# A transformer pair on one core: the second block's projections as four 2x2 block products of seven half-size products each

## The reference, cut to what matters

```
h = modulate(rmsnorm(x, norm1_g), sh_a, sc_a)             # 512 x 1024
proj = h @ w_in                                            # 1024 x 2080
q, k, v, g, a_low, p = split(proj, [256, 512, 1024, 1536, 1568])
la = log_sigmoid(a_low @ w_dec + b_dec) / 16               # decay, two directions
o = gated linear attention of q, k, v with la, in both directions
o = rmsnorm(o) * silu(g)
pooled = ((window mean - identity) of p) @ w_pool, scaled, for windows 2, 4, 8, 16
out = concat(o, pooled) @ w_out
```

## Time and profile before

| what | value |
|---|---|
| median of 3 timed runs | 1575.39 us (1570.91 to 1577.83) |
| span of the profiled execution, first to last instruction | 1569.6 us |
| own time of the profiled execution beside its span | not listed apart; the timed runs lie 1.3 to 8.3 us above the span |
| TensorE busy | 1407.1 us, 90% of the span |
| VectorE, ScalarE, GpSimd busy | 46%, 24%, 24% |
| mean granted TensorE clock | 0.977 |
| the stage of the change, 1005 to 1150 us: TensorE busy | 140.6 of 145 us |

### The profile page before, as it was taken

One profiled execution on the slowest core, in us unless ns is written; L12 is line 12 of the kernel. 1 busy time (PEld: TensorE's weight loads), 2 busy tenths in 40 slices (PEclk: granted clock), 3 DMA queues, 4 the chain that ended last, 5 costly groups with the idle time before them and its releaser, 6 DMA issues. The chain is left out here.

```text
span 1569.6 us, 21971 instructions
## 1 busy us (share of the span) xinstructions
PE 1407.1 (90%) x8518; PEld 948.7 (60%) x8518; DVE 717.6 (46%) x1222; ACT 375.2 (24%) x775; POOL 375.1 (24%) x293
## 2 busy tenths in 40 slices
PE   5998998999999989989999999999988977988781
PEld 4864444886454458778888868874667863333230
DVE  5261435124549977687615153500364464332224
ACT  3313445203343333332210032401231010000001
POOL 2420002620005525644545532000000011111110
PEclk9999999999999999999999999999999979999996
DMA  5238220123112114315242312421134169999995
GB/s 195 69 98 272 76 58 24 54 81 107 54 55 81 54 56 161 110 57 203 79 160 86 103 54 63 102 71 54 30 109 160 56 257 382 422 425 423 425 382 219
DMA packets 119831, 232.57 MB, mean 148 GB/s; under 512 B 13361, under 2 KB 103055, under 8 KB 110515
## 3 DMA queue, kind: packets, MB, share of 16 engines
q1 hardware_dynamic: 114403, 220.54, 39.0%
q0 software_dynamic: 5184, 8.55, 1.5%
q10 hardware_dynamic: 144, 2.10, 0.3%
HBM read 223.66 MB, written 17.84 MB: 154 GB/s over the span
## 5 line engine op out<-in xcount | busy, mean ns | idle before, releaser
L991 PE MATMUL psv<-arena 128*128 128x256 f32 x1328 | 291.6, 379 | 2.5 <-issue 2.5
L991 PEld LDWEIGHTS psv<-arena 128*128 128x128 f32 x1328 | 251.7, 190 | 39.1 <-issue 5.2
L953 PE MATMUL psv<-arena,wslot 128*128 128x512 f32 x384 | 170.8, 598 | 0.5 <-issue 0.5
L2322 DVE TENSOR_TENSOR arena<-arena,psv 128x512 f32<-128x512 f32 x82 | 56.4, 688 | 224.0 <-PE psv L991 222.1
L1589 PE MATMUL pss<-arena 128*64 128x512 f32 x432 | 119.4, 621 | 16.5 <-DMA arena<-w_expert_in 12.7
L953 PEld LDWEIGHTS psv<-arena,wslot 128*128 128x128 f32 x384 | 71.1, 190 | 84.0 <-issue 83.7
L1681 ACT ACTIVATE arena<-pss 128x512 f32<-128x512 f32 (+2 forms) x130 | 74.3, 571 | 193.7 <-PE pss L953 130.0
L953 PE MATMUL pss<-arena 128*128 128x512 f32 x224 | 99.6, 597 | 7.1 <-ACTq L155 4.5
L2537 DVE SCALAR_TENSOR_TENSOR arena<-psv,ccols,arena 128x510 f32<-128x510 f32 (+1 forms) x96 | 71.9, 749 | 52.8 <-ACT arena L1851 49.5
L1589 PEld LDWEIGHTS pss<-arena 128*64 128x64 f32 x432 | 36.8, 143 | 72.1 <-issue 72.1
L991 PE MATMUL psv<-arena,wslot 128*128 128x256 f32 x320 | 72.5, 381 | 6.1 <-ACT arena L1730 2.5
(11 more groups left out here) (362 smaller groups left out, 2150.4 us busy)
## 6 DMA issues: line engine op xcount, KB each, us to landing
arena<-w_expert_in SPq DMA_DIRECT2D x25, 2048.0 KB, 25.7
arena<-w_expert_out SPq DMA_DIRECT2D x32, 1024.0 KB, 29.6
wslot<-w_in SPq DMA_DIRECT2D x28, 1024.0 KB, 5.5
wslot<-w_ada SPq DMA_DIRECT2D x19, 1024.0 KB, 6.3
arena<-w_in SPq DMA_DIRECT2D x14, 1024.0 KB, 6.9
wslot<-w_expert_in SPq DMA_DIRECT2D x5, 2048.0 KB
arena<-w_ada SPq DMA_DIRECT2D x5, 1024.0 KB, 8.9
arena<-x SPq DMA_DIRECT2D x8, 512.0 KB, 7.5
```

What stands on the lines that cost most here:

```text
L953: m = mm(o, l, r, start=(n == 0), stop=(n == len(pairs) - 1))
L991: m = mm(o[:, j * HALF_T:(j + 1) * HALF_T], l[:, c, j * P:(j + 1) * P], r[:, c, :], start=new and j == 0 and c == 0, stop=j == 1 and c == ...
L2322: L.did(V.tensor_tensor(o, x, y, ALU.add), *sig)
```

## The change

The eight blocks are regrouped into four pairs: k with the first half of v (unit 17), the second half of v with the first half of p (unit 18), both of g (unit 19, feature-major), q with the second half of p (unit 20). Each runs through `seven` with the new buffers `part_c`, `held_c`, `term_c`. q leaves token-major into `q2tok` and is transposed by TensorE into `q2T`, as k was before. The activations' four terms are made by VectorE. a_low has its own buffer `wa2` and its load, ahead of the weight blocks, and runs behind unit 17; the decay matmuls run behind unit 20. The sums of weights for unit 17 straddle phase 4 on GpSimd: two of them before it, the in-place one behind it, since the context tiles still read that block. The `wdec` memset moves behind `last_part(17)`.

```diff
+        term_c = [at(B + (16 + 4 * n) * K, 4, HALF_T) for n in range(4)]
+        part_c = [at(147 * K, 4, WC), at(151 * K, 4, WC), at(115 * K, 4, WC)]
+        held_c = [at(119 * K + n * SEQ, 2, HALF_T) for n in range(4)]
+        wa2 = at(155 * K, KC, 32)
+        q2tok = at(24 * K, NT, WC)
...
-        for key, col, n in (("k2", O2_K, 256), (("v2", 0), O2_V, 256), (("v2", 1), O2_V + 256, 256), ("q2", O2_Q, 256),
-                            (("g2", 0), O2_G, 256), (("g2", 1), O2_G + 256, 256), ("a2", O2_A, 32),
-                            (("p2", 0), O2_P, 256), (("p2", 1), O2_P + 256, 256)):
-            stream(key, w2, col, n)
+        for key, col in ((("kv2", 0), O2_K), (("kv2", 1), O2_V), (("vp2", 0), O2_V + WC), (("vp2", 1), O2_P),
+                         (("g2", 0), O2_G), (("g2", 1), O2_G + WC), (("qp2", 0), O2_Q), (("qp2", 1), O2_P + WC)):
+            stream(key, w2, col, WC)
...
+        def corner_c(v, u, j, n):
+            o, c = {17: ((k2, 0), (v2, 0)), 18: ((v2, WC), (p2, 0)), 20: ((q2tok, 0), (p2, WC))}[u][j]
+            return o[:, 2 * n:2 * n + 2, c:c + WC]
...
-            stream_to("q2")
+            load(wa2, w2[:, O2_A:O2_A + 32].rearrange("(c p) n -> p c n", p=P), "ld_a2")
+            stream_to(("vp2", 1))
```

TensorE's list:

```diff
-            for t in range(NT):
-                L.need(s["h2_ready"])
-                L.need(s["half_ready"])
-                token_tile("s", wk, t, h2T)
-            used()
-            for t in range(NT):
-                token_tile("v", wv, t, h2T)
-            used()
-            L.need(s["k2_ready"], NT)
+            L.need(s["h2_ready"], 2)
+            L.need(s["half_ready"], 2)
+            seven(17, h2T, part_c, term_c, True, by_token=True, w=[wk, wv])
+            L.need(s["h2_ready"], 2)
+            L.need(s["half_ready"], 2)
+            pe.wait_ge(s["ld_a2"], 16)
+            for src, n in ((h2T, SEQ), (hcT, CTX)):
+                strips(bank("v"), wa2, src, n).then_inc(s["full_v"], 1)
+            pe.wait_ge(s["corner_ready"], 14)
+            pe.wait_ge(s["raw_ready"], 3 * 17 + 2)
             for j in range(2):
                 turn("s", [k2[:, t, j * P:(j + 1) * P] for t in range(NT)])
...
+            seven(18, h2T, part_c, term_c, by_token=True, w=[wv1, slot(("vp2", 1))])
+            seven(19, h2T, part_c, term_c)
+            seven(20, h2T, part_c, term_c, by_token=True)
+            pe.wait_ge(s["corner_ready"], 17)
+            pe.wait_ge(s["raw_ready"], 3 * 20 + 2)
             for j in range(2):
-                feature_tile("s", w, j, h2T)
...
+                turn("s", [q2tok[:, t, j * P:(j + 1) * P] for t in range(NT)])
+            pe.wait_ge(s["ld_small"], 16 * 10)
+            L.need(s["a2_ready"], 2)
+            for t in range(NT + NTC):
+                mm(bank("v"), a2T[:, t * P:(t + 1) * P], wdec, start=True, stop=True).then_inc(s["full_v"], 1)
+
+            pe.wait_ge(s["raw_ready"], 3 * 21)
```

GpSimd's list:

```diff
                 L.did(TT(part[0], a21, a22, ALU.add), s["part_ready"])
                 L.did(TT(part[1], part[0], a11, ALU.subtract), s["part_ready"])
+                unused()
                 L.did(TT(a21, a11, a21, ALU.subtract), s["part_ready"])
...
-            phase(4)
+            parts(17, part_c, lambda: phase(4))
+            last_part(17, part_c)
             nc.gpsimd.memset(wdec, 0.0).then_inc(s["wdec_zero"], 1)
+            for u in range(18, 21):
+                parts(u, part_c)
+                last_part(u, part_c)
```

VectorE's list, up to the end of unit 17:

```diff
-            for b2 in range(2):
-                for t in range(NT):
-                    b = full()
-                    L.did(V.tensor_copy(v2[:, t, b2 * 256:(b2 + 1) * 256], b[:, 0:256]), s["free_v"])
+            dve.wait_ge(s["half_ready"], 3 * NT + NTC)
+            term(term_c[0], quarter(h2T, 0, 1), quarter(h2T, 0, 0))
+            term(term_c[1], quarter(h2T, 1, 1), term_c[0])
+            term(term_c[2], quarter(h2T, 1, 1), quarter(h2T, 0, 1))
+            term(term_c[3], quarter(h2T, 1, 0), term_c[1])
+            add_second(17, held_c)
+            recombine(17, held_c, None, corner_c)
```

More of the change, by code:

```diff
@@ L470, in build @@
             half_ready row_ready sq_ready on_ready dz_ready mixT_ready sums_ready
[L471 to L472 removed]
+            x1_ready x1T_ready pinT_ready x2_ready mod_ready h2_ready hc_ready mT_ready
+            ld_a2 k2_ready a2_ready absz_ready lz_ready la_ready bexp_ready qb_ready kexp_ready kst_ready
             sprev_ready sc_ready o2_ready sq2_ready rt2_ready cat_ready x3_raw x3_ready h3_ready lg_ready
@@ L611, in build @@
                  ("dz", 0), ("dz", 2), ("gd", 0), ("gd", 2), ("brd", 0), ("brd", 2),
[1 row of a table removed]
[2 rows of a table added]
         SEVEN_JOB = [4, 7, 10, 14, 17, 20, 23, V_ON, V_ON + 3, V_ON + 14, V_ON + 17, V_ON + 20, V_ON + 23,
-                     V_ON + 26, V_ON + 29, V_ON + 32 + NT, V_ON + 35 + NT + NTC]
+                     V_ON + 26, V_ON + 29, V_ON + 32 + NT, V_ON + 35 + NT + NTC,
+                     V_ON + 38 + 2 * NT + 3 * NTC, V_ON + 43 + 2 * NT + 3 * NTC, V_ON + 46 + 2 * NT + 3 * NTC,
+                     V_ON + 49 + 2 * NT + 3 * NTC]
         TERM_SET = [("q", 0)] * 3 + [("h", 0)] * 2 + [("h", 1)] * 2 + [("q", 1)] * 4 + [("h", 2)] * 2 + \
-                   [("h", 3)] * 2 + [("h", 4)] * 2
+                   [("h", 3)] * 2 + [("h", 4)] * 2 + [("q", 2)] * 4
         def seven_slots(u):
@@ L682, in by4 @@
             return v.rearrange("p (h n) -> p h n", h=4)
-        S_NORM = 267
+        S_NORM = 259
         def chunk_at(d, n):
@@ L822, in _ @@
                          a["w_decay_2"][0, d], "ld_small")
-            stream_to(("p2", 1))
+            stream_to(("qp2", 1))
             for g in range(2, 4):
@@ L972, in token_tile, with seven @@
                     .then_inc(s["full_" + r], 1)
-            def seven(u, x, part, term, first=False, by_token=False, lower=lambda: None):
-                n = at_slot[0]
-                assert [n, n + 1] == seven_slots(u), (u, n)
+            def seven(u, x, part, term, first=False, by_token=False, lower=lambda: None, w=None):
                 assert jobs["v"] == SEVEN_JOB[u], (u, jobs["v"])
-                w = [slot((SEVEN[u][0], SEVEN[u][1] + j)) for j in range(2)]
+                if w is None:
+                    assert [at_slot[0], at_slot[0] + 1] == seven_slots(u), (u, at_slot[0])
+                    w = [slot((SEVEN[u][0], SEVEN[u][1] + j)) for j in range(2)]
                 a11, a12, a22 = w[0][:, 0:4, :], w[0][:, 4:8, :], w[1][:, 4:8, :]
@@ L1342, in _ @@
             L.need(s["half_ready"], NTC)
-            wk, wv = slot("k2"), slot(("v2", 0))
+            wk, wv = slot(("kv2", 0)), slot(("kv2", 1))
             for t in range(NTC):
@@ L1347, in _ @@
                 token_tile("v", wv, t, hcT)
-            wv1 = slot(("v2", 1))
+            wv1 = slot(("vp2", 0))
             for t in range(NTC):
@@ L1368, in _ @@
-            used()
-            w = slot("q2")
-            for j in range(2):
-                feature_tile("s", w, j, h2T)
[L1372 to L1393, removed]
@@ L1987, in _ @@
                 turned(h2T, t, gain[:, 0:8], mod[:, 0:8, 0])
-            for t in range(NT):
-                evict(k2[:, t, :], 256, "k2_ready")
+            hold_first(17, held_c)
+            corner_of(17, None, ACT.Copy, corner_c)
+            hold_third(17, held_c)
             for j in range(2):
                 evict(k2T[:, j, :], SEQ, "k2_ready")
+            hold_first(18, held_c)
+            hold_third(18, held_c)
+            corner_of(18, None, ACT.Copy, corner_c)
+            hold_first(19, held_c)
+            hold_third(19, held_c)
+            corner_of(19, g2T, ACT.Silu)
+            others_of(19, g2T, ACT.Silu, None)
+            hold_first(20, held_c)
+            hold_third(20, held_c)
+            corner_of(20, None, ACT.Copy, corner_c)
             for j in range(2):
                 evict(q2T[:, j, :], SEQ, "k2_ready", ACT.Copy, scale=DK2 ** -0.5)
-            for j in range(4):
-                evict(g2T[:, j, :], SEQ, "k2_ready", ACT.Silu)
             for t in range(NT + NTC):
@@ L2130, in weights_in, with parts @@
                 return w
-            def parts(u, part):
+            def parts(u, part, unused=lambda: None):
                 w = weights_in(u)
@@ L2800, in _ @@
                 L.did(V.tensor_copy(a2T[:, c0:c0 + n], b[:, 0:n]), s["a2_ready"], [s["free_v"]])
[L2801 to L2812, removed]
+            add_second(18, held_c)
+            recombine(18, held_c, None, corner_c)
+            add_second(19, held_c)
+            recombine(19, held_c, g2T)
+            add_second(20, held_c)
+            recombine(20, held_c, None, corner_c)
+            dve.wait_ge(s["ld_small"], 16 * 10)
+            for t in range(NT + NTC):
+                z = la[:, t, :]
+                b = full()
+                add(z, b, bdec, s["free_v"])
+                L.did(V.scalar_tensor_tensor(zabs[t], z, -1.0, z, ALU.mult, ALU.max), s["absz_ready"])
```

2 lines of the change are left out of this document (removed), and 3 rows, old and new, of the table SEVEN.

## The result

The changed kernel takes 1562.9 us (median of 12 runs, 1557.5 to 1569.0), the kernel before 1571.8 (12 runs, 1569.0 to 1577.8, the three shown ahead of the prediction among them). The ratio is 0.9947, 95% interval 0.9935 to 0.9960: 8.3 us gained, 6.3 to 10.2. Of the 4.9, 3.5 is the starting point: the three runs shown ahead of the prediction had a median of 1575.39, all twelve have 1571.8.

What follows compares the result with a forecast made beforehand. TensorE's instruction issue was taken to bound the stage. -14.94 + 3.62 + 0.92 + 1.7 + 0.90 + 0.2 = -7.6, from a median of 1575.4 to 1567.8 us; range 1562.5 to 1573, and the measured time was 4.9 below the forecast.

Steps and rivals of the forecast that it cites:

- First term: TensorE's issue in the stage: four units of 112 instructions, 99.24 us, replace eight plain blocks, 114.18; -14.94.
- Rival (e): Units 17 to 20: half products save nothing because sums of weights come late; no change, 1575; 0.09 together with (d).
- Second term: Start of unit 17: delayed as GpSimd's sums hold up VectorE's shift additions; +3.62, between +1.8 and +6.0.
- Rival (b): Start of unit 17: shift additions not held up, 1.8 delay, clock stays up; -11.1, 1564.3; chance 0.12.
- Third term: Inside unit 17: the corner waits for ScalarE's copy, 4.37 us where a half product takes 3.46; +0.92.
- Fourth term: Start of unit 17: TensorE's clock falls to 1.2 GHz after some 3.5 us idle; +1.7, between 0 and twice that.
- rival (a): Start of unit 17: the clock stays up despite the idle time; -9.3, 1566.1; chance 0.24.
- Smaller terms: Rest of the stage: q's two transposes +0.90, waits +0.2; strips, k transposes and decay matmuls moved, not changed.
- The +0.2 for waits: Rest of the stage: small waits of TensorE added and removed by the regrouping, put at +0.2.
- The tail: Decay chain behind unit 20, under the pooling: 3.3 us of slack before the third pooling copy; cost 0, one for one beyond.
- Rival (c): Uncovered tail: VectorE's third pooling copy misses its 3.3 us slack; 6 us more gives 1570.5; chance 0.13, slower 0.04.
- rival (d): Behind the stage: the experts' stage, bound by transfers, swallows the gain; 1575.4; 0.09 together with (e).

Runs made afterwards that it cites:

- e2: Changed kernel with unit 19 (the g columns) put back to two plain blocks of four feature tiles; 1564.9 us, ratio 0.9953 to the kernel before.
- e1: Changed kernel with GpSimd's two sums behind phase 4 made to wait for VectorE's four terms; 1560.5 us, ratio 0.9939 to the kernel before.
- e5: Changed kernel with all four GpSimd sums of unit 17 behind phase 4 instead of two; 1567.0 us in one run.
- e10: e4 with GpSimd's two sums running right behind phase 4 again; 1558.9 us, ratio 0.9923 to the kernel before.
- e4: e1 plus context strip ahead of the transposes, last context tile behind them, three context copies ahead of the normalisation; 1554.3 us, ratio 0.9890.
- e3: Changed kernel with ten result-neutral 128x512 copies on ScalarE between exponents and logarithms; 1568.6 us, ratio 0.9974 to the kernel before.
- e6: Changed kernel with TensorE waiting for all four VectorE differences before unit 17; 1570.8 us, ratio 0.9989 to the kernel before.
- e8: The changed kernel itself, unaltered, timed and profiled once more; 1562.0 us, ratio 0.9923 to the kernel before.

## Why the prediction was right, and where it was not

**First term, -14.94: right.** In the place of the eight blocks stand units 18 to 20 of 24.7 to 24.8 each and unit 17, 1014.07 to 1040.01, of 25.9 with its corner's wait; e2 puts one back and pays 3.68. That is a reading of the traces; e2's timed runs are too few to tell 3.7 from nothing. Rival (e) is out: the only gap inside a unit is the corner's in unit 17.

**Second term, +3.62: right in size and cause.** In the kernel before, the first block started 1005.13 - 1001.61 = 3.52 behind the first transpose; after, unit 17 starts 7.15 behind it, 3.63 later. e1 takes the sums away, and the additions' delay goes; e5 doubles the sums, and twice as many additions are held; e10 puts them back into e4, and 1.2 of waiting comes back. Rival (b) is out. The Trainium skill, page "SBUF — State Buffer", section "SBUF: two separate sides", has this exclusion for whole instructions, and these runs agree: held additions, otherwise of 0.69, end 0.54 or 0.55 behind the sum, whatever part of it was left when they were issued. The upper bound that stood beside the 3.62 was added up wrongly: +6.0 is one whole sum more, and one for each of the two additions would be +8.3. What the prediction didn't see is that there were two limits so near each other: with VectorE freed, ScalarE's fourth tile sets the corner and takes 0.48 of the 1.8 back.

**Third term, +0.92: right.** The corner starts 1018.54 - 1014.07 = 4.47 behind the first half product, where the next one starts 3.56 behind it, without a wait: 0.91.

**Fourth term, +1.7 for the clock: mis-sized.** A fall costs 2.7 to 2.9, not 1.7, since most of the sixteen matmuls of the first half product run slow (3.46 more would be all of them at half speed). It came in 3 of 6 profiles, where I had held it likelier than not; six are too few to call that chance wrong. The mean of that is 1.4, near the 1.7 by luck. The changed kernel's own profile was rival (a), the one without the fall: -9.83 against its -9.3, and the clock of 0.5 that was to show the forecast is not in it. The timed 8.3, 6.3 to 10.2, cannot tell the forecast's 7.6 from that rival's 9.3. The Trainium skill, page "TensorE: Matmul & The Clock Gate", section "HAM oscillation — how this bites in real kernels", has the fall behind a long enough gap; these runs agree at 12.1 us and give it one time in two at 3.46.

**Smaller terms.** The q transposes cost 1118.84 - 1117.94 = 0.90, as said. The +0.2 for waits was wrong by 0.5: without the clock the sum says -9.3 and the stage -9.83. The rows tell the pieces: the +0.2 did not come, and the moved work was not unchanged but 0.4 cheaper. The strips now take 1042.73 - 1040.01 = 2.72, where the 3.07 of before held a wait of 0.28 for VectorE, and the decay matmuls 5.15 where they took 5.23.

**The tail: right.** Slack 3.3 foreseen, 3.0 to 3.1 measured. "One for one beyond" holds for the wait (e3: 3.55 for 6.6 of copies), but not for the price: behind the wait the clock fell, and that cost 2.3 more in e3's profile. Rival (c) is not what happens, but it is a real cliff: it begins 3.1 us away.

**The end: rival (d) is out.** At the same clock the whole kernel is 10.0 +- 1.3 shorter, the stage 9.9. Nothing is swallowed behind it.

What stays open is why the clock falls in one run and not in the next behind the same idle time, and whether the timed runs, of which there is no trace, fell as often as the profiled ones.

## What to carry to other kernels

When helpers' work is moved next to an eviction that gates TensorE, look for operations of VectorE with both operands in SBUF: here each was held until the running sum was over (0.69 became 1.75 to 2.05), and moving the sums some us later costs nothing if they have slack. An idle time of TensorE is best filled with its own work from ahead of the wait (e10: 2.2 us for the filling by itself), and with 1.7 us of idle time or less the clock fell in none of four profiles. When an engine is freed, ask which other one is due next to it; here it was 0.5 us behind.

## What the hardware did that I had not expected

The same kernel's runs differ by 10 us and more, and the mean granted clock goes with a good part of it: 1.03 +- 0.16 us more for each 0.001 less of mean clock over all timed runs, which brings the spread within a kernel from 3.3 us (standard deviation) to 2.1. The changed kernel's runs go from 1557.5 at 0.977 to 1568.8 at 0.967, and this is more than the whole change is worth. A term of some us is therefore read from the stage in the trace, or at the same clock.

GpSimd suffers from the exclusion too, a little: its first sum takes 2.37 and the next ones, while an addition of VectorE stands in front, 2.67 to 2.68.

The clock can be down before work starts, in e6 from 1013 on and in e8 from 1008.5, and what that costs depends on how soon it is back. In e6 it was at 1.00 again by 1023.0, 3.3 us after TensorE had started, and 1.5 was lost; in e8 by 1015.0, 6.0 us after, and 2.9 was lost. In e3's tail it was at 0.50 until 1148, 7 us after the gates had begun, some of it idle, and 2.3 was lost.
